# The first projection tile computed in two halves of 256 tokens, with its weights loaded after the first token tile

## The chip, the cores and the metric

The kernel runs on one core of a Trainium2 chip. The metric is the device time of one launch in microseconds (us), median of three runs. A core has TensorE (PE; its weight loads are a row of their own, PEld), VectorE (DVE), ScalarE (ACT), GpSimd (POOL) and SyncE (SP). Each works through its own instructions in order and meets the others only at semaphores. SP here does nothing but issue DMAs.

## The reference

One layer of a decoder trunk on 512 tokens of width 1024. The stretch that the change touches is the very beginning: the norm of x and the first columns of the combined input projection.

```python
def rms_norm(x, g):
    xf = x.astype(jnp.float32)
    y = xf * lax.rsqrt(jnp.mean(xf * xf, axis=-1, keepdims=True) + NORM_EPS)
    return (y * g.astype(jnp.float32)).astype(x.dtype)
...
        h = rms_norm(x, norm_pre_mix[l])
        proj = h @ w_in[l]
        p_rwkv, p_nsa, p_swa, p_gate = _split(proj, (RWKV_COLS, NSA_COLS, SWA_COLS, GATE_COLS))
```

Behind it come three token mixers, an output projection, and a SwiGLU network. All of that is the same before and after.

## The kernel before

**Numbers.** Every dense product is done in three passes. A float32 operand is split into a high part (rounded to the matmul's format) and a low part (the rest): weights WRAW into WHI and WLO, the scaled and transposed x into HHI and HLO. A projection tile is 128 output columns for all 512 tokens: 8 chunks k of the inner dimension, and for each chunk WHI x HHI ("x_high"), WHI x HLO ("x_low") and WLO x HHI ("low"), 24 matmuls in all, which add up in one bank of PSUM. `steps(n)` issues n chunks' worth (3 matmuls each) of the list of tiles, JOBS.

**x.** x arrives as four tiles of 128 tokens (XTOK0[:, t], 512 KB each, semaphore x_in[t]). PE transposes each in 8 blocks of 128x128 (`x_transpose(t, k)`, a product with the identity that lies in CONP). Chunk k of all four token tiles fills bank k of PSUM. The norm's 1/rms is not applied here but to the results, so the products can start on unnormalised x. ACT then writes HHI[k] = high part of (bank k times the gain g_pre_mix), DVE writes HLO[k] = the rest, both 128x512 (ACT L904, DVE L1462), and PE multiplies.

**The gains** come as rows (PRAW) and are turned into columns by two transposes and two DVE copies (L1457, L1458) into PARC. ACT and DVE need them before the first HHI and HLO (semaphore prow_ok).

**Sums of squares** for the norm: x tiles 0 and 2 on ACT (L894), 1 and 3 on DVE (L1452); then a square root, a reciprocal (L1467), four small products (L1469), and one PE product (L2358) that stands in the middle of projection tile 1.

**Order on the queues.** SP issues x tiles 0, 1, 2, then the weights of projection tile 0, then x tile 3, then the weights of tile 1 and small constants. PE transposes tiles 0 to 2 (7 of 8 blocks each), the gains, then 10 transposes of the identity that nobody reads (KEEP_BUSY, they keep the engine working while x tile 3 is on its way), then tile 3, then the eighth block of all four, then the 24 matmuls of tile 0. ACT makes the high part of tile 0's weights (L888), POOL the low part (L773); for tile 1 POOL makes both (POOL_HI, L777). DB[0] and DB[1] (banks 0 and 1) hold the projection tiles in turn, R is the other six banks.

## Time and profile before

| | |
|---|---|
| three runs | 1001.74, 1001.81, 1001.84 us, median 1001.81 |
| profiled execution | 1001.6 us, of it the span between first and last instruction 999.8 us |
| PE busy | 983.0 us (98% of the span) |
| DVE, POOL, ACT busy | 692.9, 452.3, 425.5 us |
| first matmul of projection tile 0 | 14.95 us after the span's start |
| first matmul of projection tile 1 | 20.50 us |

A profile's row names line, engine, operation, output<-inputs and shape. A busy PE says little by itself, since matmuls are pipelined: what counts is when each batch of them starts, and what released it. The change lies in the first 21 us.

### The profile page before, as it was taken

The page shows a single profiled execution, that of the slowest core. Times are in us where ns is not written, and L with a number is a line of the kernel's source. Part 1 is how long each engine was busy: PE and PEld are TensorE (multiplying, and loading weights), DVE is VectorE, ACT ScalarE, POOL GpSimd, SP SyncE. Part 2 cuts the span into 40 slices and gives each one's busy share as a digit, 9 for nine tenths or more (in the row PEclk, how much of TensorE's full clock was granted, in tenths as well). Part 3 has the DMA queues.
Part 4 walks back from the last instruction along what each step waited for, and adds up shares of the span by engine and source line. Part 5 has one row for each costly group of instructions (what it writes and reads, how often), then busy time and mean ns, then how long its engine had stood idle before and what let it go on. Part 6 is the DMA issues. An engine that isn't in the chain of part 4 may idle for free.

```text
span 999.8 us, 19627 instructions
## 1 busy us (share of the span) xinstructions
PE 983.0 (98%) x7920; PEld 799.7 (80%) x7920; DVE 692.9 (69%) x1160; ACT 425.5 (43%) x829; POOL 452.3 (45%) x511
## 2 busy tenths in 40 slices
PE   6999999999999999999999999999999999999997
PEld 5787777777777777777778888888889998888886
DVE  3799796565566956546556882269887865489987
ACT  4134432322314334546555444545444443345563
POOL 3366557254334766656683448446222234510000
PEclk9999999999999999999999999999999999999999
DMA  9345533122223564112113636433322333244452
GB/s 262 89 129 151 122 92 68 24 65 65 67 66 98 157 159 137 49 50 56 52 54 122 193 116 229 131 127 106 106 85 86 112 106 109 86 136 170 157 176 99
DMA packets 149459, 111.48 MB, mean 112 GB/s; under 512 B 21190, under 2 KB 132048, under 8 KB 149369
## 3 DMA queue, kind: packets, MB, share of 16 engines
q1 hardware_dynamic: 145644, 104.16, 35.7%
q10 hardware_dynamic: 3692, 6.07, 2.2%
q8 instruction: 63, 1.03, 0.4%
q14 instruction: 28, 0.22, 0.1%
q0 software_dynamic: 32, 0.00, 0.0%
HBM read 99.70 MB, written 10.52 MB: 110 GB/s over the span
## 4 chain that ended last, share of the span: by engine, by line
PE 86%; DVE 10%; issue 1%; DMA 1%; POOL 1%; ACT 1%; SPq 0%; DVEq 0%; ACTq 0%
PE ps L2318 33%; PE ps L2798 5%; PE ps L2797 5%; PE ps L2802 5%; PE ps L2332 4%; PE ps L2438 3%; PE ps L2683 3%; PE ps L2858 2%; PE ps L2860 2%; PE ps L2859 2%; PE ps L2625 2%; PE ps L2835 2%; PE ps L2832 2%; PE ps L2831 2%; DVE XF L1430 2%
## 5 line engine op out<-in xcount | busy, mean ns | idle before, releaser
L2318 PE MATMUL ps<-HLO,WHI 128*128 128x512 f32 x440 | 178.2, 405 | 0.4 <-issue 0.4
L2318 PE MATMUL ps<-HHI,WHI 128*128 128x512 f32 x440 | 175.5, 399 | 1.0 <-DVE HLO L1462 0.7
L773 POOL TENSOR_TENSOR WLO<-WRAW,WHI 128x1024 fp32r<-128x1024 f32 (+1 forms) x52 | 104.2, 2006 | 106.5 <-ACT WHI L888 106.5
L869 POOL TENSOR_TENSOR WLO<-WRAW,WHI 128x512 fp32r<-128x512 f32 x50 | 72.3, 1453 | 118.8 <-ACT WHI L1230 117.5
L2318 PE MATMUL ps<-HHI,WLO 128*128 128x512 f32 x440 | 118.1, 398 | 0.0
L777 POOL CAST WHI<-WRAW 128x256 fp32r<-128x256 f32 (+1 forms) x133 | 62.7, 472 | 106.5 <-PE ps L2318 106.3
L808 POOL TENSOR_TENSOR WLO<-WRAW,WHI 128x256 fp32r<-128x256 f32 x132 | 105.6, 800 | 10.7
L2318 PEld LDWEIGHTS ps<-HHI,WHI 128*128 128x128 f32 x440 | 82.6, 188 | 23.2 <-issue 4.7
L2318 PEld LDWEIGHTS ps<-HLO,WHI 128*128 128x128 f32 x440 | 82.6, 188 | 22.7 <-issue 5.1
L2318 PEld LDWEIGHTS ps<-HHI,WLO 128*128 128x128 f32 x440 | 80.5, 188 | 18.3 <-issue 1.4
L2798 PE MATMUL ps<-HLO,WHI 128*128 128x512 f32 x200 | 77.9, 389 | 0.0
L2797 PE MATMUL ps<-HHI,WHI 128*128 128x512 f32 x200 | 77.9, 389 | 0.0
L888 ACT ACTIVATE WHI<-WRAW 128x1024 fp32r<-128x1024 f32 (+1 forms) x51 | 43.5, 854 | 71.7 <-PE ps L2318 67.3
L1073 ACT ACTIVATE EB<-EB,STAT 128x257 f32<-128x257 f32 (+5 forms) x96 | 50.4, 526 | 49.5 <-DVE STAT L1809 42.3
L1230 ACT ACTIVATE WHI<-WRAW 128x512 fp32r<-128x512 f32 x69 | 43.0, 629 | 65.7 <-PE ps L2802 42.1
L2802 PE MATMUL ps<-HHI,WLO 128*128 128x512 f32 x200 | 53.5, 389 | 0.0
L837 POOL TENSOR_SCALAR EB<-EB,STAT,GLT 128x128 f32<-128x128 f32 (+3 forms) x64 | 38.6, 615 | 29.2 <-DVE STAT L1825 29.1
L2802 PEld LDWEIGHTS ps<-HHI,WLO 128*128 128x128 f32 x200 | 37.5, 188 | 7.8
L2797 PEld LDWEIGHTS ps<-HHI,WHI 128*128 128x128 f32 x200 | 37.6, 188 | 7.7
L2798 PEld LDWEIGHTS ps<-HLO,WHI 128*128 128x128 f32 x200 | 37.6, 188 | 7.7
L1832 DVE COPY PTB<-ps 128x512 f32<-128x512 f32 (+3 forms) x36 | 20.6, 572 | 32.2 <-PE ps L2332 32.2
L1809 DVE CUSTOM_DVE_ANT_0 EB<-ps,TB 128x128 f32<-128x128 f32 (+3 forms) x64 | 28.2, 488 | 19.2 <-PE ps L2625 16.9
(517 smaller groups left out, 2404.1 us busy)
## 6 DMA issues: line engine op xcount, KB each, us to landing
WRAW<-in_w_in SPq DMA_DIRECT2D x47, 512.0 KB, 4.4
WRAW<-in_w_gate SPq DMA_DIRECT2D x22, 512.0 KB, 3.8
WRAW<-in_w_up SPq DMA_DIRECT2D x22, 512.0 KB, 3.9
WRAW<-in_w_down SPq DMA_DIRECT2D x19, 512.0 KB, 3.4
spilled<-SQ SPq DMA_DIRECT2D x24, 256.0 KB, 2.4
GATES<-spilled SPq DMA_DIRECT2D x6, 768.0 KB, 4.8
WRAW<-in_w_in SPq DMA_DIRECT2D x16, 256.0 KB, 3.7
WRAW<-in_w_branch SPq DMA_DIRECT2D x32, 128.0 KB, 2.9
```

What stands on the lines that cost most here:

```text
L773: return pool.tensor_tensor(lo[:, 0:chunks, :], WRAW[:, n % NRAW, 0:chunks, :], hi[:, 0:chunks, :].bitcast(F32), ALU.subtract)
L777: return pool.tensor_copy(WHI[:, slot_of(n), k0:k1, :], WRAW[:, n % NRAW, k0:k1, :])
L808: lo = pool.tensor_tensor(WLO[:, slot_of(n), k:k + 2, :], WRAW[:, n % NRAW, k:k + 2, :], WHI[:, slot_of(n), k:k + 2, :].bitcast(F32), ALU. ...
L869: pool.tensor_tensor(lo, raw_half(item[1], item[2]), hi.bitcast(F32), ALU.subtract).then_inc(w_lo, 1)
L888: act.activation(split_of(n)[0][:, 0:width_of(n), :], WRAW[:, n % NRAW, 0:width_of(n), :], ACT.Copy).then_inc(w_hi, 1)
L1073: last = act.activation(EB[:, n % 3, g, cols], EB[:, n % 3, g, cols], ACT.Exp, scale=-1.0, bias=st[:, 0, u:u + 1], accum_out=st[:, 1, u:u ...
L1230: act.activation(item_slot(m)[0], raw, ACT.Copy).then_inc(w_hi, 1)
L2318: last = pe.matmul(DB[g % 2][:, :], (wlo if which == "low" else whi)[:, c, :], lo if which == "x_low" else hi, start=a == 0, stop=a == 3 * ...
L2332: return pe.transpose(dst, src, ident[0:n, 0:n])
L2797: pe.matmul(dst, hi[:, kk, :], HHI[:, k, :], start=k == 0, stop=False)
L2798: pe.matmul(dst, hi[:, kk, :], HLO[:, k, :], start=False, stop=False)
L2802: last = pe.matmul(dst, lo[:, kk, :], HHI[:, k, :], start=False, stop=k == 7)
```

## The change

Projection tile 0 is computed in two halves: columns 0 to 255 (tokens of x tiles 0 and 1), then columns 256 to 511 (x tiles 2 and 3).

- `x_chunk(h, k)` places chunk k of half h: two chunks share a bank (k and k+4), half 0 in banks 2 to 5, half 1 in 6, 7, 1, 2. All HHI and HLO operations become 128x256, 16 on each engine where there were 8 of 128x512. ACT's for k of 4 and more wait for DVE's of k-4 (the bank's other chunk).
- SP issues x tile 0, the weights of tile 0, then x tiles 1, 2, 3, then the weights of tile 1.
- POOL makes the high part of tile 0's weights too (POOL_HI = [0, 1]); ACT no longer does.
- DVE's square of x tile 1 stands behind the gain copies, ACT's square of x tile 2 behind all 16 HHI.
- PE: 8 transposes of x tile 0, the gains, 8 of x tile 1, the 10 idle ones, x_high and x_low of chunks 0 to 4 of half 0, 8 transposes of x tile 2, chunks 5 to 7, the 8 low products of half 0, 8 transposes of x tile 3, and the 24 matmuls of half 1 with 256 columns each.

```diff
@@ -139,7 +139,7 @@
 NRAW, NSPL = 4, 2
 
 PIECE0 = NS0 + 5
-POOL_HI = [1]
+POOL_HI = [0, 1]
 KEEP_BUSY = 10
 
 SPILLED = list(range(SW0, GC0))
@@ -497,6 +497,9 @@
     psum = [nc.alloc_psum_tensor(f"ps{n}", [P, T], F32) for n in range(8)]
     DB, R = psum[0:2], psum[2:8]
     DB4 = [DB[0], DB[1], R[0], R[1]]
+
+    def x_chunk(h, k):
+        return psum[((2, 3, 4, 5), (6, 7, 1, 2))[h][k % 4]][:, 256 * (k // 4):256 * (k // 4) + 256]
 
     def head_cols(n, jj, sink=0):
         w = keys_of(n) + sink
@@ -676,10 +679,11 @@
             def x_tile(t):
                 sp.dma_start(XTOK0[:, t, :], x[t * P:(t + 1) * P, :]).then_inc(x_in[t], 16)
 
-            for t in range(3):
-                x_tile(t)
+            x_tile(0)
             for n in range(FF0):
                 if n == 1:
+                    x_tile(1)
+                    x_tile(2)
                     x_tile(3)
                 if n == 2:
                     sp.dma_start(HOT[:, :], hot).then_inc(hot_in, 16)
@@ -896,12 +900,13 @@
 
             x_square(0)
             act.wait_ge(xsq_ok, 1)
+            act.wait_ge(prow_ok, 2)
+            for h in range(2):
+                for k in range(KC):
+                    act.wait_ge(*((xT_done, KC * h + 2 * k + 2) if k < 4 else (xlo_ok, KC * h + k - 3)))
+                    act.activation(HHI[:, k, 256 * h:256 * h + 256], x_chunk(h, k), ACT.Identity,
+                                   scale=par("g_pre_mix", k)).then_inc(xhigh_ok, 1)
             x_square(2)
-            hi_part(0)
-            act.wait_ge(prow_ok, 2)
-            for k in range(KC):
-                act.wait_ge(xT_done, k + 1)
-                act.activation(HHI[:, k, :], psum[k][:, :], ACT.Identity, scale=par("g_pre_mix", k)).then_inc(xhigh_ok, 1)
             act.wait_ge(xsq_ok, 2)
             act.wait_ge(xsum_ok, 2)
             act.activation(XRINV, XSS, ACT.Sqrt, scale=1.0 / D, bias=EPSC[:, 0:1]).then_inc(norm_std, 1)
@@ -1452,15 +1457,17 @@
                 dve.tensor_tensor_reduce(TMP[:, 0:2, :].rearrange("p a t -> p (a t)"), XTOK0[:, t, :], XTOK0[:, t, :],
                                          1.0, 0.0, ALU.mult, ALU.add, XSS[:, t:t + 1]).then_inc(xsum_ok, 1)
 
+            dve.wait_ge(prow_T, 1)
+            dve.tensor_copy(PARC[:, 0:NPAR1], DB[0][:, 0:NPAR1]).then_inc(prow_ok, 1)
+            dve.tensor_copy(PARC[:, NPAR1:NPAR1 + NPAR2], DB[0][:, P:P + NPAR2]).then_inc(prow_ok, 1)
             x_square(1)
-            dve.wait_ge(prow_T, 1)
-            dve.tensor_copy(PARC[:, 0:NPAR1], R[5][:, 0:NPAR1]).then_inc(prow_ok, 1)
-            dve.tensor_copy(PARC[:, NPAR1:NPAR1 + NPAR2], R[5][:, P:P + NPAR2]).then_inc(prow_ok, 1)
             dve.wait_ge(prow_ok, 2)
-            for k in range(KC):
-                dve.wait_ge(xhigh_ok, k + 1)
-                dve.scalar_tensor_tensor(out=HLO[:, k, :], in0=psum[k][:, :], scalar=par("g_pre_mix", k),
-                                         in1=HHI[:, k, :].bitcast(F32), op0=ALU.mult, op1=ALU.subtract).then_inc(xlo_ok, 1)
+            for h in range(2):
+                for k in range(KC):
+                    cols = slice(256 * h, 256 * h + 256)
+                    dve.wait_ge(xhigh_ok, KC * h + k + 1)
+                    dve.scalar_tensor_tensor(out=HLO[:, k, cols], in0=x_chunk(h, k), scalar=par("g_pre_mix", k),
+                                             in1=HHI[:, k, cols].bitcast(F32), op0=ALU.mult, op1=ALU.subtract).then_inc(xlo_ok, 1)
             dve.wait_ge(xsum_ok, 1)
             x_square(3)
             dve.wait_ge(norm_std, 1)
@@ -2279,10 +2286,6 @@
             def products_of(n):
 
                 ks = range(JOBS[n][3])
-                if n == 0:
-                    late = [("low", k - 2) for k in range(2, len(ks) + 2)]
-                    early = [[("x_high", k), ("x_low", k)] for k in ks]
-                    return early[0] + early[1] + sum(([late[k - 2]] + early[k] for k in ks[2:]), []) + late[-2:]
                 return [(part, k) for k in ks for part in ("x_high", "x_low")] + [("low", k) for k in ks]
 
             def steps(count):
@@ -2309,10 +2312,6 @@
                         for a in range(3 * k, 3 * k + 3):
                             which, c = order[a]
                             hi, lo = rhs(n, c)
-                            if n == 0 and which == "x_low":
-                                pe.wait_ge(xlo_ok, c + 1)
-                            if n == 0 and which == "x_high":
-                                pe.wait_ge(*((xhigh_ok, c + 1) if c else (xlo_ok, 1)))
                             if a == first_low:
                                 pe.wait_ge(w_lo, n + 1)
                             last = pe.matmul(DB[g % 2][:, :], (wlo if which == "low" else whi)[:, c, :],
@@ -2334,25 +2333,51 @@
 
             pe.wait_ge(con_in, 16)
             def x_transpose(t, k):
-                return tr(psum[k][:, t * P:(t + 1) * P], XTOK0[:, t, k * P:(k + 1) * P])
-
-            for t in range(3):
-                pe.wait_ge(x_in[t], 16)
-                for k in range(KC - 1):
-                    x_transpose(t, k)
+                at0 = P * (t % 2)
+                return tr(x_chunk(t // 2, k)[:, at0:at0 + P], XTOK0[:, t, k * P:(k + 1) * P])
+
+            def first_high(h, k):
+                cols = slice(256 * h, 256 * h + 256)
+                pe.wait_ge(xhigh_ok, KC * h + k + 1)
+                pe.matmul(DB[0][:, cols], split_of(0)[0][:, k, :], HHI[:, k, cols], start=k == 0, stop=False)
+                pe.wait_ge(xlo_ok, KC * h + k + 1)
+                pe.matmul(DB[0][:, cols], split_of(0)[0][:, k, :], HLO[:, k, cols], start=False, stop=False)
+
+            def first_low(h, k):
+                cols = slice(256 * h, 256 * h + 256)
+                return pe.matmul(DB[0][:, cols], split_of(0)[1][:, k, :], HHI[:, k, cols], start=False, stop=k == KC - 1)
+
+            pe.wait_ge(x_in[0], 16)
+            for k in range(KC):
+                x_transpose(0, k)
             pe.wait_ge(par_in, 32)
-            tr(R[5][:, 0:NPAR1], PRAW[0:NPAR1, 0, :], NPAR1)
-            tr(R[5][:, P:P + NPAR2], PRAW[0:NPAR2, 1, :], NPAR2).then_inc(prow_T, 1)
+            tr(DB[0][:, 0:NPAR1], PRAW[0:NPAR1, 0, :], NPAR1)
+            tr(DB[0][:, P:P + NPAR2], PRAW[0:NPAR2, 1, :], NPAR2).then_inc(prow_T, 1)
+            pe.wait_ge(x_in[1], 16)
+            for k in range(KC):
+                x_transpose(1, k // 2 + 4 * (k % 2)).then_inc(xT_done, 1)
             for n in range(KEEP_BUSY):
-                tr(psum[n % (KC - 1)][:, 3 * P:4 * P], ident)
+                tr(x_chunk(1, n % 3)[:, 0:P], ident)
+            pe.wait_ge(w_hi, 1)
+            pe.wait_ge(prow_ok, 2)
+            for k in range(5):
+                first_high(0, k)
+            pe.wait_ge(x_in[2], 16)
+            for k in range(KC):
+                x_transpose(2, k)
+            for k in range(5, KC):
+                first_high(0, k)
+            pe.wait_ge(w_lo, 1)
+            for k in range(KC):
+                first_low(0, k)
             pe.wait_ge(x_in[3], 16)
-            for k in range(KC - 1):
-                x_transpose(3, k).then_inc(xT_done, 1)
-            pe.wait_ge(prow_ok, 2)
-            for t in range(4):
-                last = x_transpose(t, KC - 1)
-            last.then_inc(xT_done, 1)
-            steps(8)
+            for k in range(KC):
+                x_transpose(3, k // 2 + 4 * (k % 2)).then_inc(xT_done, 1)
+            for k in range(KC):
+                first_high(1, k)
+                last = first_low(1, k)
+            last.then_inc(dense_done, 1)
+            dense["n"] = 1
             steps(4)
             pe.wait_ge(diag_ok, 4)
             pe.matmul(R[4][:, :], ones, SSUM[:, :], start=True, stop=True).then_inc(norm_ss, 1)
```

How the instructions of three queues stand now. SP before, from its first DMA: XTOK are the x tiles, WRAW the raw weights of a projection tile.

```order
L677 DMA XTOK_83<-in_x 128x1024 x3
L711 DMA WRAW<-in_w_in 128x8x128
L677 DMA XTOK_83<-in_x 128x1024
L711 DMA WRAW<-in_w_in 128x8x128
L685 DMA HOT<-in_hot 33x1024
```

SP after, at the same place:

```order
L680 DMA XTOK_83<-in_x 128x1024
L715 DMA WRAW<-in_w_in 128x8x128
L680 DMA XTOK_83<-in_x 128x1024 x3
L715 DMA WRAW<-in_w_in 128x8x128
L689 DMA HOT<-in_hot 33x1024
```

The first weights moved from the fourth place to the second; x tiles 1 and 2 stand one place later, x tile 3 and everything behind it where it was. PE before, from the third x tile to the first matmuls of projection tile 0 (a transpose is a MATMUL with CONP):

```order
L2332 MATMUL ps<-CONP,XTOK_83 128x128 [waits x_in2]
L2332 MATMUL ps<-CONP,XTOK_83 128x128 x6
L2332 MATMUL ps<-CONP,PRAW 128x74 [waits par_in]
L2332 MATMUL ps<-CONP,PRAW 128x64
L2332 MATMUL ps<-CONP 128x128 x10
L2332 MATMUL ps<-CONP,XTOK_83 128x128 [waits x_in3]
L2332 MATMUL ps<-CONP,XTOK_83 128x128 x6
L2332 MATMUL ps<-CONP,XTOK_83 128x128 [waits prow_ok]
L2332 MATMUL ps<-CONP,XTOK_83 128x128 x3
L2318 MATMUL ps<-HHI,WHI 128x512 [waits xlo_ok,w_hi]
L2318 MATMUL ps<-HLO,WHI 128x512 [waits xlo_ok]
```

PE after, from the second x tile to the second half's first matmuls:

```order
L2331 MATMUL ps<-CONP,XTOK_83 128x128 [waits x_in1]
L2331 MATMUL ps<-CONP,XTOK_83 128x128 x7
L2331 MATMUL ps<-CONP 128x128 x10
L2342 MATMUL ps<-HHI,WHI 128x256 [waits xhigh_ok,prow_ok,w_hi]
L2344 MATMUL ps<-HLO,WHI 128x256 [waits xlo_ok]
...
L2331 MATMUL ps<-CONP,XTOK_83 128x128 [waits x_in2]
L2331 MATMUL ps<-CONP,XTOK_83 128x128 x7
...
L2348 MATMUL ps<-HHI,WLO 128x256 [waits w_lo]
L2348 MATMUL ps<-HHI,WLO 128x256 x7
L2331 MATMUL ps<-CONP,XTOK_83 128x128 [waits x_in3]
L2331 MATMUL ps<-CONP,XTOK_83 128x128 x7
L2342 MATMUL ps<-HHI,WHI 128x256 [waits xhigh_ok]
```

Half 0's products stand between the transposes, so the transposes of x tiles 2 and 3 wait their turn behind products. DVE after, its first operations:

```order
L1461 COPY PARC<-ps 128x74 [waits prow_T,con_in]
L1462 COPY PARC<-ps 128x64
L1457 ISA TMP,MISC<-XTOK_83 128x1024 [waits x_in1]
L1457 ISA MISC 128x1
L1469 SCALAR_TENSOR_TENSOR HLO<-ps,PARC,HHI 128x256 [waits xhigh_ok,prow_ok]
L1469 SCALAR_TENSOR_TENSOR HLO<-ps,PARC,HHI 128x256 [waits xhigh_ok] x15
L1457 ISA TMP,MISC<-XTOK_83 128x1024 [waits x_in3,xsum_ok]
```

The square of x tile 1 (the ISA row) now stands behind the copies and directly ahead of 16 HLO operations.

## Rows read from the trace of the kernel before

**Rows 1.** The page: busy time per engine, the clock's slices, the last chain

```profile
PE 983.0 (98%) x7920; PEld 799.7 (80%) x7920; DVE 692.9 (69%) x1160; ACT 425.5 (43%) x829; POOL 452.3 (45%) x511
PEclk9999999999999999999999999999999999999999
PE 86%; DVE 10%; issue 1%; DMA 1%; POOL 1%; ACT 1%; SPq 0%; DVEq 0%; ACTq 0%
```

**Rows 2.** The chain that ended last, 0 to 24 us: start us, us, what

```profile
2.84 9.93 DMA XTOK<-in_x
...
12.82 0.34 PE ps L2332
...
13.25 0.70 ACT HHI L904
...
14.05 0.76 DVE HLO L1462
...
14.95 8.43 PE ps L2318 x36
```

**Rows 3.** Timeline, SP's queue: start us, us the issue took, queue, line, what

```profile
0.74 1.34 SPq L677 DMA_DIRECT2D XTOK<-in_x  x3
2.12 0.68 SPq L711 DMA_DIRECT2D WRAW<-in_w_in  x1
2.84 2.30 SPq L677 DMA_DIRECT2D XTOK<-in_x  x1
```

**Rows 4.** Timeline, PE's weight loads: start, length of the batch, [idle before <-releaser]

```profile
6.14 1.35 PEld L2332 LDWEIGHTS ps<-CONP,XTOK 128*128 128x128 f32 x7 [6.14 <-DMA CONP<-in_con]
7.93 1.34 PEld L2332 LDWEIGHTS ps<-CONP,XTOK 128*128 128x128 f32 x7 [0.43 <-DMA XTOK<-in_x]
9.64 0.75 PEld L2332 LDWEIGHTS ps<-CONP,XTOK 128*128 128x128 f32 x7 [0.37 <-DMA XTOK<-in_x]
10.36 0.40 PEld L2332 LDWEIGHTS ps<-CONP,PRAW 74*128 74x128 f32 x2
10.83 1.07 PEld L2332 LDWEIGHTS ps<-CONP 128*128 128x128 f32 x10
```

**Rows 5.** Timeline, ACT and POOL: weights of tile 0 and 1

```profile
11.47 1.06 ACT L888 ACTIVATE WHI<-WRAW 128x1024 fp32r<-128x1024 f32 x1 [0.63 <-DMA WRAW<-in_w_in]
...
12.61 2.35 POOL L773 TENSOR_TENSOR WLO<-WRAW,WHI 128x1024 fp32r<-128x1024 f32 x1 [10.64 <-ACT WHI L888]
15.15 1.04 POOL L777 CAST WHI<-WRAW 128x1024 fp32r<-128x1024 f32 x1 [0.19 <-DMA WRAW<-in_w_in]
```

**Rows 6.** Timeline, DVE, 8 to 22 us

```profile
8.04 1.22 DVE L1452 CUSTOM_DVE_ANT_0 TMP<-XTOK 128x1024 f32<-128x1024 f32 x1 [7.13 <-DMA XTOK<-in_x]
...
14.05 5.36 DVE L1462 SCALAR_TENSOR_TENSOR HLO<-ps,PARC,HHI 128x512 fp32r<-128x512 f32 x8 [2.74 <-ACT HHI L904]
19.33 1.21 DVE L1452 CUSTOM_DVE_ANT_0 TMP<-XTOK 128x1024 f32<-128x1024 f32 x1
...
21.19 0.87 DVE L1469 TENSOR_SCALAR SSUM<-CONP,MISC 128x128 f32<-128x128 f32 x4
```

**Rows 7.** Timeline, PE: start of projection tile 1, and the norm's product

```profile
20.50 0.39 PE L2318 MATMUL ps<-HHI,WHI 128*128 128x512 f32 x1
...
23.22 1.02 PE L2358 MATMUL ps<-SSUM,CONP 128*128 128x512 f32 x2
```

**Rows 8.** The same operations with 256 columns at the second norm, 650 to 661 us

```profile
650.99 0.28 PE L2762 MATMUL ps<-HLO,XWHI 128*128 128x256 f32 x1
651.11 0.28 PE L2763 MATMUL ps<-HHI,XWLO 128*128 128x256 f32 x1
...
656.51 3.03 ACT L1163 ACTIVATE HHI<-ps,PARC 128x256 fp32r<-128x256 f32 x8 [3.74 <-PE ps L2332]
...
657.39 3.23 DVE L1909 SCALAR_TENSOR_TENSOR HLO<-ps,PARC,HHI 128x256 fp32r<-128x256 f32 x8 [4.01 <-ACT HHI L1163]
```

**Rows 9.** DMA packets of ACT's queue (q10), 9.00 to 9.25 us: packets, MB, share

```profile
q10 hardware_dynamic: 2, 0.00, 0.9%
```

## The prediction

> **What bounds the kernel now.** I read the page first, for who is busy and what the last chain is made of; then that chain over the first 24 us; then the timelines of SP's queue, PE's weight loads, ACT, POOL and DVE over the same stretch; and last the second norm, near 650 us, where the kernel already does with 256 columns what the change now does at the start. PE is busy for 98% of the span and holds 86% of the last chain [rows 1], so from the first projection tile on, the program runs at PE's pace, and whatever moves the first matmul of projection tile 1 moves the end by about as much. That matmul starts at 20.50 [rows 7]; it is the one number of this prediction. Ahead of it the chain is [rows 2]: x tile 3 is in flight until 12.8, PE transposes, ACT makes HHI from 13.25, DVE HLO from 14.05, PE's products run from 14.95 without a gap. So before, the start hangs on the landing of x tile 3, and then 24 matmuls of 512 columns take 20.50 - 14.95 = 5.55 us, of which half could have been done ahead of it. That is what the change goes for. The question is whether anything else has become later.
>
> **Landings.** The change makes the start hang on x tile 1 instead, since half 0 needs tiles 0 and 1. Before, x tiles 0 to 3 are met at about 6.0, 7.9, 9.6 and 12.8 [rows 2, 4], tile 0's weights at 11.47 and tile 1's at 15.15 [rows 5]. SP's order now has the weights second [rows 3]. The queue delivers in its order and each piece has 512 KB, so I give the places their old times: weights about 8.0, x tile 1 about 9.65, x tile 2 about 11.3, x tile 3 and tile 1's weights as before. In small pieces the weights take a little longer than an x tile (9.64 to 11.47 is 1.83 us, 7.93 to 9.64 is 1.71 [rows 4, 5]), so x tile 1 stands at 9.75. Bounds: 9.3 if the lighter start of the queue helps, 10.1 if the weights delay it as much again. The gains come on ACT's queue, whose last packets pass at about 9.2 [rows 9]; PE wants them at 7.8 now (before: 10.36 [rows 4]). They must be there ahead of x tile 1, and are; at worst this costs 0.2 us.
>
> **Weights.** POOL's cast takes 1.04 us and its low part 2.35 [rows 5]: from 8.1 that gives a high part at 9.2 and a low part at 11.6. PE wants them at 11.6 and near 15. Both are covered; the low part has 3 us to spare. The cast of 1.06 us goes from ACT and costs nothing on POOL, which sat idle.
>
> **Half 0.** DVE's square of x tile 1 comes first: 0.1 after landing and 1.25 us with its read-out (8.04 to 9.27 [rows 6]), so DVE is free at 11.1. ACT has HHI of chunk 0 long before, by my count at 10.3 to 10.9. HLO with 256 columns: 8 of them take 3.23 us [rows 8], the last one counted whole (0.48), so the pitch is 0.39. They halve in width but not in time (5.36 us for 8 of 512 columns [rows 6], pitch 0.66): 16 of them cost 6.3 us of DVE where 8 cost 5.4. The fifth, chunk 4, starts at 11.1 + 4 x 0.39 = 12.7, ends 13.15, and PE has its product 0.16 later (14.05 + 0.74 to 14.95 [rows 2], the row's 0.76 rounded): 13.3. Only now come the 8 transposes of x tile 2, 0.107 each when the clock is up (0.75 us for 7 [rows 4]): 14.2. Chunks 5 to 7, six matmuls at 0.12 [rows 8], with the last HLO ready at 14.5: 14.9. Eight low products: 15.85. Then x tile 3 is transposed, though it has lain there since 12.8.
>
> **Half 1.** From the first transpose to ACT is 0.43 us (12.82 to 13.25 [rows 2]); ACT now waits for two, which adds 0.11: 16.4. From ACT's start to DVE's: 0.88 at the second norm, where DVE waits for two ACT operations (pitch 0.37); one less gives 0.51 [rows 8]: 16.9. DVE starts its eighth at 16.9 + 7 x 0.39 = 19.65, ends 20.13; 0.16 to PE, 0.12 each for x_low and low: projection tile 1 starts at 20.55. Before: 20.50. **The sum is +0.05 us.** What half 0 wins is spent on three things: 1.25 us of DVE's square that stands in the way, 0.9 us more of HLO time, and DVE's idle time between its halves (14.3 to 16.9), in which PE, in order, finishes half 0 before it gives ACT anything to do.
>
> **What is late next.** The norm's product wants DVE's four small operations. They end at 22.06 and PE comes for them at 23.2 [rows 6, 7]. DVE leaves HLO at 20.13 instead of 19.41, so they end at about 22.8: 0.4 us of slack is left, no cost. ACT's square of x tile 2 (1.2 us) now runs at 19.3 and is done ahead of DVE's of tile 3 (21.3). POOL's high part of tile 1 waits for a landing that does not move.
>
> **The clock.** This is the open term. The page shows a granted clock of full speed (2.4 GHz) everywhere [rows 1], yet the first and second batch of 7 transposes take 1.35 and 1.34 us and the third 0.75 [rows 4]: PE starts at about half its pace (the 1.2 GHz level) and rises between 9.3 and 9.6, after 14 transposes with one pause of 0.43 us. Now it does 8 transposes, the gains, and then sits from about 8.3 to 9.75, a pause of 1.4 us that was not there. If it rises all the same by then, the sum stands. If it does not, 8 transposes of x tile 1 end at 11.3 instead of 10.6, which DVE doesn't notice, and the ten idle ones end at 13.2 instead of 11.7. PE then has ten matmuls to catch up on, 1.2 us: 14.4 instead of 13.3, and everything behind moves by 1.1 us. Each further us at the slow pace behind 13.2 costs about half a us more. The ten idle transposes are free at full pace and in the way at half pace.
>
> On this the Trainium skill, "TensorE: Matmul & The Clock Gate", Part 4 (PE-mode transpose), has a rule against the change: transposes do not bring the clock up, since they don't count as PE work in the same way. By it PE would stay slow until its first real matmuls. The third batch [rows 4] speaks against it: only transposes had gone before, and it runs at the fast pitch. So I don't build on the rule, but it would make the slow case the longer one.
>
> **Rivals.**
> 1. The clock comes up late (after the idle transposes begin, by about 14): +1.1 us, up to +1.7, so 1002.9 to 1003.6. For it: the new pause right where the clock used to rise. Against: PE has by then worked about as long as before its pause. Chance 0.27.
> 2. It stays slow through half 0's products, and the kernel is slower by more than 2 us. The point is a rise later than about 15.0: 1.1 + (15.0 - 13.2) / 2 = 2.0. Slow until half 0 is done (8 transposes x 0.19, 24 matmuls x 0.24 by doubling [rows 4, 8] from 13.2 make 20.5 instead of 15.85) would be +4.7, 1006.5. Also here: x tile 1 landing beyond 10.5 together with rival 1. Chance 0.12.
> 3. x tile 1 lands early (9.3) and the hand-overs between engines are somewhat shorter than I took them: -0.5 to -1, 1000.9 to 1001.4. Chance 0.10.
> 4. DVE doesn't have to wait between its halves, so that it is bound by itself: 11.1 + 15 x 0.39 + 0.48 = 17.4, plus 0.4: projection tile 1 at 17.8, a gain of 2.7 us, 999.1. PE's order speaks against it: x tile 3's transposes stand behind all of half 0. It would need PE to be far ahead of DVE there, and the row pitches don't give that. Chance 0.06.
>
> **How the numbers follow.** The profiled execution took 1001.6 us, 1.8 of it outside the span of 999.8; the median of three is 1001.81, 0.2 above it. 1001.81 + 0.05, with a term of 0.05 for the gains' wait: 1001.9. That is no change, with 0.45, and its own range is 1001.4 to 1002.4 (x tile 1 at 9.3 or 10.1 is -0.4 or +0.35). For 8 in 10 I take in rival 3 and most of rival 1: 1000.9 to 1003.5. A measurement here can tell about 0.2%, or 2 us, from no change. Faster than 999.8: rival 4, 0.06. Slower than 1003.8: rival 2, 0.12. Within: 0.82.
>
> **What would show it.** Right: x tile 1's transposes start near 9.7; DVE's first HLO near 11.1 and its ninth near 16.9, with an idle gap of over 2 us between eighth and ninth that ends on ACT; x tile 3's transposes start near 15.9 without waiting for a DMA; projection tile 1 near 20.5; the norm's product waits for nothing. The clock: a batch of 8 transposes of x tile 1 in 0.85 us says it is up, 1.5 us says it is not. Wrong: DVE's ninth HLO before 15.5 or after 18.5; a wait of PE for w_lo or w_hi; a wait for the gains that holds up x tile 1; or a shift at 20.5 us that differs from the one at the end by more than 0.5 us, which would mean that the rest of the program does not follow PE's start.

## The result: slower by a quarter of a per cent

| | before | after |
|---|---|---|
| median of 21 runs | 1001.81 us | 1004.56 us |
| lowest to highest | 1001.14 to 1002.97 | 1002.16 to 1006.05 |
| ratio, 95% interval | | 1.0024, 1.0018 to 1.0030 |
| profiled execution, span | 1001.6, 999.8 us | 1006.05, 1004.2 us |

The forecast was 1001.9 with a range of 1000.9 to 1003.5, so the measured time lies outside. It has the size of rival 2 (slower by more than 2 us, 0.12), but not its mechanism, as the clock will show. The profiled execution of after is its slowest of 21; more than half of the loss in its trace is not in every run, as will be seen. The times of after spread over 3.9 us where those of before spread over 1.8, and they gather in two places: ten between 1002.2 and 1004.0, eleven between 1004.6 and 1006.1.

The page of after differs from before's [rows 1] by 24 matmuls and by little else:

```profile
PE 986.5 (98%) x7944; PEld 803.7 (80%) x7944; DVE 696.3 (69%) x1168; ACT 425.7 (42%) x836; POOL 452.6 (45%) x512
```

The timeline has it. First DVE and POOL of after, 8 to 22 us (start us, us, engine, line; in brackets the idle time before and what ended it):

```profile
9.55 3.30 DVE L1457 CUSTOM_DVE_ANT_0 TMP<-XTOK 128x1024 f32<-128x1024 f32 x1
12.78 0.08 DVE L1457 DVE_READ_ACCUMULATOR2_ANT MISC<- 128x1 f32 x1
12.78 3.22 DVE L1469 SCALAR_TENSOR_TENSOR HLO<-ps,PARC,HHI 128x256 fp32r<-128x256 f32 x8
18.68 3.24 DVE L1469 SCALAR_TENSOR_TENSOR HLO<-ps,PARC,HHI 128x256 fp32r<-128x256 f32 x8 [2.68 <-ACT HHI L907]
```

```profile
8.30 1.03 POOL L781 CAST WHI<-WRAW 128x1024 fp32r<-128x1024 f32 x1 [6.33 <-DMA WRAW<-in_w_in]
9.42 2.35 POOL L777 TENSOR_TENSOR WLO<-WRAW,WHI 128x1024 fp32r<-128x1024 f32 x1
```

DVE's square of x tile 1 took 3.30 us where the same operation took 1.22 before [rows 6]. It was issued 0.13 us behind POOL's subtraction, which ran from 9.42 to 11.77, and ended about 1.1 us behind that one's end: it looks as if it had begun only when POOL was done. A later run speaks for that reading: with 9 tiny transposes ahead of x tile 1 (below) the square was issued 0.30 us behind POOL's subtraction instead of 0.13, took 0.17 us less, and ended as long behind POOL's end:

```profile
9.78 3.13 DVE L1457 CUSTOM_DVE_ANT_0 TMP<-XTOK 128x1024 f32<-128x1024 f32 x1
```

```profile
9.48 2.35 POOL L777 TENSOR_TENSOR WLO<-WRAW,WHI 128x1024 fp32r<-128x1024 f32 x1
```

HLO starts at 12.78 instead of the forecast 11.1. Then PE's weight loads of after:

```profile
9.57 1.57 PEld L2331 LDWEIGHTS ps<-CONP,XTOK 128*128 128x128 f32 x8 [0.74 <-DMA XTOK<-in_x]
11.12 2.15 PEld L2331 LDWEIGHTS ps<-CONP 128*128 128x128 f32 x10
13.25 0.34 PEld L2342 LDWEIGHTS ps<-HHI,WHI 128*128 128x128 f32 x1
...
14.54 0.28 PEld L2342 LDWEIGHTS ps<-HHI,WHI 128*128 128x128 f32 x1
14.74 0.19 PEld L2344 LDWEIGHTS ps<-HLO,WHI 128*128 128x128 f32 x1
...
15.11 0.90 PEld L2331 LDWEIGHTS ps<-CONP,XTOK 128*128 128x128 f32 x8
```

Against before's third batch, 7 in 0.75 us [rows 4], these 8 took 1.57 and the idle ten 2.15: PE was at its slow pace (the 1.2 GHz level) until about 14.6, though the page shows the clock as full in every slice. The forecast had one pause of 1.4 us ahead of x tile 1. There are two, of 0.94 us ahead of the gains (7.38 to 8.32) and of 0.74 us ahead of x tile 1 (8.83 to 9.57). There as forecast is DVE's gap between the halves (2.68 us, forecast 2.6). Last, PE of after at the two places that rows 7 show of before:

```profile
22.32 0.40 PE L2317 MATMUL ps<-HHI,WHI 128*128 128x512 f32 x1
...
25.05 1.02 PE L2383 MATMUL ps<-SSUM,CONP 128*128 128x512 f32 x2
```

Projection tile 1 is late by 22.32 - 20.50 = 1.82 us. The span is longer by 4.4. So 2.6 us more arise behind it, and the waits of PE in after (for whom, on whom: us in total, times, longest) between 150 and 320 us say where:

```profile
PE ps L2463 <- issue: 2.3, 5, 0.6
PE ps L2331 <- DVE BK L1656: 0.8, 3, 0.4
```

"issue" is idle time that nothing in the profile ended. Before had two such groups there:

```profile
PE ps L2438 <- issue: 0.7, 2, 0.4
PE ps L2318 <- issue: 0.4, 1, 0.4
```

### The profile page after: what moved, and what is told of

It reads as the page before. It is cut to its first block, busy times and chain, and to the rows that moved or that the text cites. A ratio compares the mean times of both kernels' runs of the same rounds, so it can differ in the third digit from the quotient of the medians.

```text
span 1004.2 us, 19691 instructions
## 1 busy us (share of the span) xinstructions
PE 986.5 (98%) x7944; PEld 803.7 (80%) x7944; DVE 696.3 (69%) x1168; ACT 425.7 (42%) x836; POOL 452.6 (45%) x512
## 4 chain that ended last, share of the span: by engine, by line
PE 86%; DVE 10%; issue 2%; DMA 1%; POOL 1%; ACT 1%; DVEq 0%; SPq 0%; ACTq 0%
PE ps L2317 32%; PE ps L2823 5%; PE ps L2822 5%; PE ps L2827 5%; PE ps L2331 4%; PE ps L2463 3%; PE ps L2708 3%; PE ps L2883 2%; PE ps L2885 2%; PE ps L2884 2%; PE ps L2650 2%; PE ps L2860 2%; PE ps L2857 2%; PE ps L2856 2%; DVE XF L1435 2%
## 5 line engine op out<-in xcount | busy, mean ns | idle before, releaser
L2317 PE MATMUL ps<-HLO,WHI 128*128 128x512 f32 x432 | 175.1, 405 | 0.0
L2317 PE MATMUL ps<-HHI,WHI 128*128 128x512 f32 x432 | 172.3, 399 | 0.3
L2317 PE MATMUL ps<-HHI,WLO 128*128 128x512 f32 x432 | 115.2, 398 | 0.0
L2823 PE MATMUL ps<-HLO,WHI 128*128 128x512 f32 x200 | 77.9, 389 | 0.0
L2822 PE MATMUL ps<-HHI,WHI 128*128 128x512 f32 x200 | 77.9, 389 | 0.0
L2827 PE MATMUL ps<-HHI,WLO 128*128 128x512 f32 x200 | 53.5, 389 | 0.0
```

The source lines that it names most:

```text
L2317: last = pe.matmul(DB[g % 2][:, :], (wlo if which == "low" else whi)[:, c, :], lo if which == "x_low" else hi, start=a == 0, stop=a == 3 * ...
L2822: pe.matmul(dst, hi[:, kk, :], HHI[:, k, :], start=k == 0, stop=False)
L2823: pe.matmul(dst, hi[:, kk, :], HLO[:, k, :], start=False, stop=False)
L2827: last = pe.matmul(dst, lo[:, kk, :], HHI[:, k, :], start=False, stop=k == 7)
```

## The experiments

Two questions: what makes projection tile 1 late (A: DVE and POOL shut each other out; B: PE's slow pace), and what makes the second part. Every kernel was timed beside before on the same chip. When the pace rises is read from the lengths of the weight loads.

### After once more

> The changed kernel again, unaltered, for a second trace of it. If the extra 2.6 us that its first trace shows between 170 and 310 us (PE idle with no releaser, 2.3 us in 5 pauses) belong to the change, they are there again; if they are chance, they differ. Both theories expect the first matmul of projection tile 1 at 22.3 us within 0.3 (20.50 before) and DVE's square of x tile 1 at 3.3 us instead of 1.2.

Measured 1004.27 us (8 runs, 1002.66 to 1005.69), ratio 1.0024 (1.0013 to 1.0034); four runs below 1004, four above. In its trace projection tile 1 starts at 22.24, the square takes 3.31 us, and the span is 1003.7. PE's pauses are there again, in nearly the same places (1.5 us of "issue"). The two traces lose the same at the start and part of the rest. But both were taken in runs of the upper group (1006.05 and 1005.49). Before's median and 1.8 us are 1003.6, and 8 of after's first 21 runs lie below 1003.6, the lowest at 1002.16: those runs lose less at the start, or gain behind it, and no trace shows which.

The pace of this second trace rises at 13.3, not at 14.6, and still projection tile 1 is no earlier. Its x_high loads come at a pitch of 0.39 us, DVE's pitch:

```profile
13.84 0.19 PEld L2342 LDWEIGHTS ps<-HHI,WHI 128*128 128x128 f32 x1
14.12 0.19 PEld L2344 LDWEIGHTS ps<-HLO,WHI 128*128 128x128 f32 x1
14.23 0.19 PEld L2342 LDWEIGHTS ps<-HHI,WHI 128*128 128x128 f32 x1
14.52 0.19 PEld L2344 LDWEIGHTS ps<-HLO,WHI 128*128 128x128 f32 x1
```

PE had caught up there and waited for the late HLO, so A alone holds the start at 22.24.

### The two causes of the late start, each alone and both

POOL's low part of tile 0 waits for DVE's square:

```diff
                 pool.wait_ge(w_hi, n + 1)
+                if n == 0:
+                    pool.wait_ge(xsum_ok, 1)
                 lo_part(n, width_of(n)).then_inc(w_lo, 1)
```

> POOL's low part of tile 0's weights waits until DVE has done its square of x tile 1. Theory A (DVE and POOL exclude each other, the square loses 2.1 us to POOL's subtraction): the square takes 1.22 us again, the first HLO starts at 11.0 instead of 12.8. Theory B (slow TensorE clock): PE never waited for HLO in half 0, since its idle transposes end at 13.3 and its first matmuls run at a pitch of 0.215, so projection tile 1 still starts at 22.3 within 0.3 and the total stays. Were A alone the cause, projection tile 1 would start at 20.6 and the total fall by 1.7 us.

Without the idle transposes:

```diff
-KEEP_BUSY = 10
+KEEP_BUSY = 0
```

> The ten idle transposes are left out. Theory B alone (they are in the way at the slow pace): projection tile 1 about 1 us earlier, at 21.2. Theory A: HLO starts at 12.8 all the same, chunk 4 of half 0 can't be done before 14.9 (15.1 now), so projection tile 1 moves by no more than 0.3 us, unless the clock now rises later and makes it worse.

> Both at once: POOL's low part waits for DVE's square, and no idle transposes. If each alone does nothing because the other bounds, the two together take off 1.2 to 1.8 us: HLO from 11.0, projection tile 1 at 20.5 to 21.1. If the clock stays slow until 14.6 or later, the gain is the smaller one or nothing.

| | square of x tile 1 | first HLO | pace rises | projection tile 1 | median | ratio |
|---|---|---|---|---|---|---|
| after | 3.30 | 12.78 | 14.6 | 22.32 | 1004.56 | 1.0024 (1.0018 to 1.0030) |
| POOL waits | 1.23 | 11.03 | 14.0 | 22.08 | 1003.05 | 1.0016 (1.0008 to 1.0025) |
| no idle transposes | 3.31 | 12.86 | about 18.9 | 24.14 | 1005.26 | 1.0032 (1.0020 to 1.0043) |
| both | 1.23 | 10.99 | 12.6 | 20.43 | 1002.56 | 1.0007 (0.9998 to 1.0016) |

DVE with both edits:

```profile
9.58 1.23 DVE L1459 CUSTOM_DVE_ANT_0 TMP<-XTOK 128x1024 f32<-128x1024 f32 x1
...
10.99 3.23 DVE L1471 SCALAR_TENSOR_TENSOR HLO<-ps,PARC,HHI 128x256 fp32r<-128x256 f32 x8 [0.18 <-ACT HHI L909]
16.80 3.23 DVE L1471 SCALAR_TENSOR_TENSOR HLO<-ps,PARC,HHI 128x256 fp32r<-128x256 f32 x8 [2.58 <-ACT HHI L909]
```

The square is 2.1 us shorter as soon as POOL doesn't subtract beside it: A is shown. By itself it moves the start by only 0.24, as B said: PE comes from its idle transposes at 13.3 and catches up at the slow pace until 14.0, so the finished HLO lie waiting for it. The median is 1.2 us below after's on the same chip (1004.27), of which the start explains 0.2; the rest belongs to the second part, and the two intervals overlap. Without the idle ones alone, projection tile 1 came 1.8 us later than in after, where 0.3 at most, or 1.1 earlier, was expected; the case that the pace rises still later was named there, but without a size. PE sits from 11.5 to 13.4, waiting for the late HLO, and its pace stays slow through nearly all of half 0:

```profile
13.39 0.29 PEld L2344 LDWEIGHTS ps<-HLO,WHI 128*128 128x128 f32 x1 [1.86 <-DVE HLO L1469]
...
15.33 1.66 PEld L2331 LDWEIGHTS ps<-CONP,XTOK 128*128 128x128 f32 x8
```

Eight transposes in 1.66 us at 15.3: that is close to the 4.7 us case of rival 2, here at +3.6. Whether the wait kept the pace slow, one trace can't say. With both edits the wait for HLO is gone too, PE works on from 11.15, and the start is 20.43, before's to 0.07 us. That is what my sum gave for a fast clock (20.55); here the clock was slow until 12.6, but the ten idle transposes were not in its way.

### The clock by itself

Idle transposes for PE in the two pauses ahead of x tile 1, on top of POOL's wait:

```diff
+            for n in range(5):
+                tr(x_chunk(1, n % 3)[:, 0:P], ident)
             pe.wait_ge(par_in, 32)
...
+            for n in range(4):
+                tr(x_chunk(1, n % 3)[:, 0:P], ident)
             pe.wait_ge(x_in[1], 16)
```

> The changed kernel with POOL's low part waiting for DVE's square, and with 5 idle transposes ahead of the gains and 4 ahead of x tile 1, in time that PE waits. Against the kernel with POOL's wait alone (projection tile 1 at 22.1) this shows the clock by itself: if PE's pace rises by 9.6 as in before, the eight transposes of x tile 1 take 0.85 us instead of 1.57, and projection tile 1 starts at 20.5 (within 0.3), a gain of 1.5 us and the number that my sum gave. If the clock was not what held it, it stays at 22.1.

```profile
9.27 0.71 PEld L2333 LDWEIGHTS ps<-CONP 128*128 128x128 f32 x4
9.97 1.45 PEld L2333 LDWEIGHTS ps<-CONP,XTOK 128*128 128x128 f32 x8
11.38 1.12 PEld L2333 LDWEIGHTS ps<-CONP 128*128 128x128 f32 x10
12.47 0.19 PEld L2344 LDWEIGHTS ps<-HHI,WHI 128*128 128x128 f32 x1
```

Projection tile 1 at 20.95, against 22.08 with POOL's wait alone: the pace is worth 1.1 us, the size of my rival 1. The pace rose not at 9.6 but near 11.1, and the four idle transposes held x tile 1 up by 0.4, so it is not the 20.5 expected. Median 1002.4, ratio 1.0003 (0.9994 to 1.0012), with one of the 11 runs, at 3057.8 us, left out: with both causes lightened, no loss can be told from before any more.

This shows what a slow pace costs, and not yet that the pauses make it slow. Seven traces of before and of its padded versions (below) have the same work on PE as far as the gains, and in them the pace rose at 9.5, 9.8, 10.5, 10.6, 10.8, 12.1 and 12.5. The third batch of transposes in two traces of one kernel (24 tiny ones, which come later), whose projection tiles 1 start at 20.71 and 21.64:

```profile
9.73 0.83 PEld L2332 LDWEIGHTS ps<-CONP,XTOK 128*128 128x128 f32 x7 [0.48 <-DMA XTOK<-in_x]
```

```profile
9.63 1.35 PEld L2332 LDWEIGHTS ps<-CONP,XTOK 128*128 128x128 f32 x7 [0.24 <-DMA XTOK<-in_x]
```

With the pauses open it rose at 12.6, 13.3, 14.0, 14.6 and 18.9, with tiny transposes in the second pause alone at 15.4, with both filled at 11.1 here and by 10.3 in the first version below, which points at the pauses. But the last version below had none longer than 0.35 us ahead of x tile 1, and there it rose near 14.4. So that the pauses delay the rise is likely, not shown.

### The second part: PE's pauses

The late start alone, in before: 34 idle transposes instead of 10. Projection tile 1 came 2.1 us late (22.64), and the median is 2.0 above before's beside it (1001.90): one to one, though single runs lie higher.

> The kernel before with 34 idle transposes instead of 10: they run to 14.5, so x tile 3 is transposed 1.65 us late and projection tile 1 starts at 22.1, nearly as in after, and PE's program is as long as that of after. If the late start passes to the end one to one, the total is 1003.5 (+1.65); if the program's length or the lateness itself brings the second part of the loss, it is 1004 to 1004.6 as after's.

Padding alone, in before: tiny transposes in the time that PE waits for x tile 3. The same edit with 12, 24 (on two chips) and 33, and one with 9 in after, ahead of x tile 1:

```diff
                 tr(psum[n % (KC - 1)][:, 3 * P:4 * P], ident)
+            for n in range(24):
+                pe.transpose(psum[n % (KC - 1)][0:32, 3 * P:3 * P + 32], ident[0:32, 0:32], ident[0:32, 0:32])
```

> The kernel before with 24 more tiny transposes (32x32) behind its ten idle ones, in time that PE waits for x tile 3 anyway: PE's program is as long as that of after, its times up to projection tile 1 are those of before (20.5, within 0.3). If the second part of the loss comes from the longer program (instructions fetched at other places), the total rises by 0.5 to 1 us; if not, it stays within 0.3 of before.

> The kernel before with 24 tiny transposes in PE's wait for x tile 3, once more. Theory C (where PE's fetched blocks of instructions begin decides about the pauses): again most runs at 1004 to 1005.2 and a few near 1001.5. If the first result was chance or that chip: one cluster near 1002.

> The same with 12: PE's program is 24 instructions longer than before's. The kernel without idle transposes (28 longer) had one tight cluster whose trace lost nothing behind the start. Theory C: one cluster, 1001.5 to 1002.2, as before. If any padding costs: between 1002.5 and 1004.

> The kernel before with 33 tiny transposes in PE's wait for x tile 3: 66 instructions longer than before, where the kernel with 24 was 48 longer and lay at 1004.1 to 1005.2 in 6 of 9 runs. They last about 1.0 us and may hold projection tile 1 up by 0.3 to 0.5 us. Theory C: 1002.1 to 1002.5, no cluster near 1004.5. If any longer program costs the same, it is 1004.5 again.

> The changed kernel with 9 tiny transposes (32x32) while PE waits for x tile 1. PE's program is 18 instructions longer than after's, 66 longer than before's, as in the kernel with POOL's wait and 9 idle transposes, whose ten undisturbed times had no second cluster. Theory C (the second part of the loss hangs on where in PE's program the fetched blocks of instructions begin): projection tile 1 at 22.3 as in after, but the times lie in one cluster near 1003.4 and the half near 1005.2 is gone. Theory D (it comes from the late start): two clusters as in after, median 1004 to 1004.6.

> The kernel before, unaltered, for a second trace of it. In the first traces the part of the time that arises behind projection tile 1 differs by kernel: after +2.6 and +2.2 us, the one with POOL's wait -0.6, without idle transposes +0.2, with both +0.5. If these pauses of PE (idle, released by nothing that the profile shows) come and go by chance, this trace differs from the first one of before by up to 1 us between 170 and 310 us with projection tile 1 at 20.5 in both; if they are fixed by the program, it doesn't.

In the traces I set the start apart from the rest: "rest" is the span less the start of the norm's product (before: 999.8 - 23.22 = 976.6), "pauses" is PE's "issue" idle between 150 and 320 us.

| kernel | PE instructions more than before | projection tile 1 | rest | pauses | median of all runs, runs above 1004 |
|---|---|---|---|---|---|
| before | 0 | 20.50 | 976.6 | 1.1 | 1001.81, 0 of 21 |
| before, second trace | 0 | 20.41 | 976.4 | 0.8 | 1001.34, 0 of 11 |
| before, 12 tiny | 24 | 20.75 | 978.4 | 1.4 | 1003.15, 2 of 11 |
| before, 24 tiny | 48 | 20.71 | 979.2 | 2.0 | 1004.32, 6 of 9 |
| before, 24 tiny, again | 48 | 21.64 | 979.9 | 2.9 | 1003.22, 4 of 11 |
| before, 33 tiny | 66 | 22.11 | 977.8 | 1.6 | 1002.52, 1 of 11 |
| before, 34 idle | 48 | 22.64 | 975.9 | 0.7 | 1003.94, 5 of 12 |
| after | 48 | 22.32 | 979.2 | 2.3 | 1004.56, 11 of 21 |
| after, second trace | 48 | 22.24 | 978.7 | 1.5 | 1004.27, 4 of 8 |
| after, 9 tiny | 66 | 22.82 | 978.2 | 1.9 | 1003.35, 4 of 11 |
| after, POOL waits | 48 | 22.08 | 976.0 | 0.5 | 1003.05, 3 of 11 |
| after, no idle | 28 | 24.14 | 976.7 | 1.0 | 1005.26, 7 of 7 |
| after, both edits | 28 | 20.43 | 977.0 | 1.3 | 1002.56, 0 of 11 |
| after, POOL waits, 9 idle | 66 | 20.95 | 976.7 | 1.3 | 1002.40, 0 of 10 |
| first version below | 66 | 19.16 | 975.6 | 0.5 | 1000.93, 0 of 10 |
| second version below | 60 | 20.80 | 977.2 | 0.7 | 1001.79, 0 of 11 |

The second trace of the padded kernel, 150 to 320 us, is the clearest:

```profile
PE ps L2440 <- issue: 2.9, 5, 0.9
PE ps L2332 <- DVE BK L1649: 0.9, 2, 0.7
```

What follows. The rest is longer where the pauses are longer, by about 1.8 us for one of pause over these 16 traces; every rest above 977.5 goes with pauses of 1.4 or more. Neither trace of before has them long, and its two rests differ by 0.2. The same kernel with nothing but 12 or 24 tiny transposes ahead has them, with its start late by no more than 0.25 us in two of the three traces, and costs 1.0013 (1.0004 to 1.0022) with 12, and 1.0016 (1.0007 to 1.0026) and 1.0013 (1.0003 to 1.0023) with 24: so neither halves nor a late start are needed for them. In the other trace (21.64) and in that with 33 (22.11) the pace rose at 12.1 and 12.5, so part of those runs' loss is a late start all the same. With 33 the ratio is 1.0007 (0.9998 to 1.0016), no clear loss, though the traced run has pauses of 1.6. A late start with 34 idle transposes mostly gives just the start (1002.4 to 1004.1 in nine of twelve runs), but has three runs of 1005.7 to 1007.3.

Theory C said that 24 instructions more cost nothing, 48 do and 66 don't. Its medians for 66 came true (1003.35 and 1002.52), but both traces have long pauses, 24 instructions cost as much as 48, and POOL's wait at 48 seldom has them: as a rule for the time it is not borne out. Theory D, the late start, fails on the padded kernels. What is shown is that a few tiny transposes more near the start of PE's program can bring up to 3 us between 170 and 310 us, in some runs and not in others. 
I took the pauses for waits for instructions to be fetched. No experiment looked at that, but the traces do: they list DMA packets of a kind "instruction", 16 KB each, on queue q8, 26 or 27 of them in this stretch, about one for every 250 of PE's instructions. Here the longest pause of the second padded trace, and the packets of q8 from 175.5 to 176.9 (packets, MB, share):

```profile
177.09 0.30 PE L2440 MATMUL ps<-AM,XX 64*64 64x64 f32 x8
178.26 0.58 PE L2440 MATMUL ps<-AM,XX 64*64 64x64 f32 x24 [0.88 <-issue]
```

```profile
q8 instruction: 1, 0.02, 5.6%
```

That packet was under way from 175.58 to 176.84, and PE went on 1.42 us later. It is so with every pause: the 16 traces have 43 of 0.2 us and more there that nothing in the profile ended, and each ends 1.19 to 1.64 us after an instruction packet is through, where a moment picked at random would do so in 8 of 100 cases. Their places go with the length of PE's program. Counted from projection tile 1, both traces of before have one at 155.6; the traces with 24 or 28 instructions more have theirs at 151 and 156, or at 156 alone; all four with 66 more have none before 236.7, and the first there. With 48 more there are two kinds, four traces with pauses at 151.1 and 155.7 (after and the kernel with 24 tiny, both traced twice) and two (34 idle, and POOL waits) with pauses at 237 and 278.6 alone. So theory C has the places right, as if they were set by where in the program a packet begins, and not the cost. What is not shown is why some of the fetches come late in one run and not in another.

### A version that tries to beat both

POOL's wait, idle and tiny transposes ahead of the gains and x tile 1, 4 idle ones behind it instead of 10, and PE's order changed so that DVE can go from half 0 to half 1 without its gap. Of its edit, the order:

```diff
+            pe.wait_ge(x_in[2], 16)
+            for k in (0, 4, 1, 5, 2, 6):
+                x_transpose(2, k)
             pe.wait_ge(w_hi, 1)
             pe.wait_ge(prow_ok, 2)
-            for k in range(5):
+            for k in range(2):
                 first_high(0, k)
-            pe.wait_ge(x_in[2], 16)
-            for k in range(KC):
+            pe.wait_ge(x_in[3], 16)
+            for k in (0, 4, 1, 5, 2, 6):
+                x_transpose(3, k).then_inc(xT_done, 1)
+            for k in range(2, 5):
+                first_high(0, k)
+            for k in (3, 7):
                 x_transpose(2, k)
+            for k in (3, 7):
+                x_transpose(3, k).then_inc(xT_done, 1)
...
-            pe.wait_ge(x_in[3], 16)
-            for k in range(KC):
-                x_transpose(3, k // 2 + 4 * (k % 2)).then_inc(xT_done, 1)
```

> A version that means to beat both: POOL's low part waits for DVE's square; short idle transposes keep PE busy ahead of the gains and of x tile 1; six of eight transposes of x tile 2 and of x tile 3 go ahead of most of half 0's products, so that DVE can go on from half 0 to half 1 without its gap of 2.6 us; padded to a program 66 instructions longer than before's. DVE alone would be done with HLO at 17.3; PE has 48 matmuls of 256 columns (5.8 us) and 16 transposes (1.7 us) from 11.2 on, so projection tile 1 starts at 18.7 to 19.6 against 20.5 before, and the total is 1000.0 to 1000.9. If the order of PE's work was not what kept DVE idle, the gap stays and it is 1001.9.

```profile
9.80 1.21 DVE L1459 CUSTOM_DVE_ANT_0 TMP<-XTOK 128x1024 f32<-128x1024 f32 x1
...
11.44 6.36 DVE L1471 SCALAR_TENSOR_TENSOR HLO<-ps,PARC,HHI 128x256 fp32r<-128x256 f32 x16 [0.42 <-ACT HHI L909]
```

```profile
19.16 0.40 PE L2319 MATMUL ps<-HHI,WHI 128*128 128x512 f32 x1
```

All 16 HLO in one run of 6.36 us, projection tile 1 at 19.16, 1.34 before before's. Median 1000.93, ratio 0.9993 (0.9983 to 1.0002): ten runs from 999.2 to 1003.4, and one at 1451.5 that is left out. The second try without idle work just ahead of x tile 1:

> As best1, but the idle transposes ahead of x tile 1 are gone (they held its transposes up until 10.3 although it lands at 9.6) and the padding stands ahead of the gains. If PE's pace rises by 10.5 as in best1, projection tile 1 starts at 18.5 (19.16 in best1) and the total is 0.6 us lower, 1000.3. If the pause ahead of x tile 1 lets the clock rise later, the transposes run at 0.19 and it starts at 19.0 to 19.8, no better than best1.

Measured 1001.79, ratio 0.9995 (0.9985 to 1.0004), from 999.0 to 1002.8; in its trace (of a run of 1002.55) tile 1 starts at 20.80, 1.0 us later than the worst that was expected. PE's pace rises only near 14.4, and DVE waits again between its halves (0.86 and 0.32 us):

```profile
9.08 0.50 PEld L2333 LDWEIGHTS ps<-CONP,PRAW 74*128 74x128 f32 x2
9.70 1.57 PEld L2333 LDWEIGHTS ps<-CONP,XTOK 128*128 128x128 f32 x8
...
14.03 0.33 PEld L2346 LDWEIGHTS ps<-HLO,WHI 128*128 128x128 f32 x1
14.30 0.73 PEld L2333 LDWEIGHTS ps<-CONP,XTOK 128*128 128x128 f32 x6
```

Both beat the changed kernel. That they beat before is likely for the first and not shown for either: the order gains 1.3 us at projection tile 1 in one trace, and in the other trace, with its late clock, nothing of that is left.

## Why the prediction was wrong, point by point

- **What bounds the kernel; the landings.** Right. x tile 1 came at 9.57 (forecast 9.75), the weights at 8.30 (8.0), tile 1's at 14.4 (15.15, earlier than I gave), the gains at 8.3. Nothing waited for weights.
- **"Both are covered": POOL's work on tile 0's weights costs nothing.** This step failed. I asked whether the result was there in time, and not what the operation does to DVE beside it. I put it at nothing. It cost the square 2.1 us and with that the first HLO 1.7, and this alone is enough for the 1.7 us at projection tile 1 (22.24 in the trace whose pace had risen by 13.3). The trace of before had the price, in a stretch that the prediction didn't use. Its chain from 46 us (start, us, what), and POOL there:

```profile
46.13 1.02 DVE XF L1430
...
47.18 2.99 DVE XF L1430
...
50.20 1.01 DVE XF L1430
```

```profile
46.60 2.77 POOL L773 TENSOR_TENSOR WLO<-WRAW,WHI 128x1024 fp32r<-128x1024 f32 x1 [3.04 <-ACT WHI L888]
```

  The same DVE operation takes 1.02 us alone and 2.99 when it meets POOL's subtraction; the one that started first went through. The Trainium skill, "SBUF — State Buffer", section "Who interferes with whom", says it outright: VectorE and GpSimd share one pair of ports, as an exclusive lock held for the whole instruction, and a VectorE operation "with two SBUF inputs" contends with a GpSimd operation that reads SBUF. The square reads x twice, and the operation at 47.18 reads NQ and PARC, which both lie in SBUF: both agree with it. HLO reads PSUM and SBUF, and it was not slowed. In before each takes 0.74 us, beside POOL's subtraction and outside of it. With POOL's wait, HLO and the subtraction start together, and both take what they take alone (8 HLO 3.23 in rows 8, the subtraction 2.35 in rows 5):

```profile
11.03 3.23 DVE L1471 SCALAR_TENSOR_TENSOR HLO<-ps,PARC,HHI 128x256 fp32r<-128x256 f32 x8 [0.18 <-ACT HHI L909]
```

```profile
11.00 2.36 POOL L777 TENSOR_TENSOR WLO<-WRAW,WHI 128x1024 fp32r<-128x1024 f32 x1 [1.60 <-DVE MISC L1459]
```

- **Half 0's and half 1's working.** Right in its pitches and hand-overs: 8 HLO in 3.22 to 3.24, DVE's gap 2.58 to 2.68 for 2.6 where HLO set the pace. The 20.43 with both edits, for 20.55, is in part luck: the pace was slow until 12.6 there and the idle transposes were missing, so it is not the case that was summed up. The order of PE was what kept DVE idle, as rival 4's argument had it: with another order the gap is gone.
- **The clock.** This term failed too. The pace rose at 14.6 and 13.3 in the two traces of after, behind the ten idle transposes both times, and a slow pace measures 1.1 us against the filled pauses. I gave it 0.27 and put the fast case, at nothing, into the sum. It should have been the other way, if only because the kernel itself spent ten transposes on keeping PE at work through a pause. Rival 2's rise beyond 15.0 was in neither trace: A and B together gave its size. The rise also varies, from 9.5 to 12.5 in the seven traces that have before's start. In before that does little harm, since PE waits for x tile 3 until 12.8 anyway. The change moved PE's work to where this variation counts.
- **The rule on transposes**. The Trainium skill, "TensorE: Matmul & The Clock Gate", Part 4 (PE-mode transpose), has it that they don't bring the clock up. In after, the pace rose within the first matmuls; but with filled pauses it rose at 11.1 with nothing but transposes before, and so it did in all seven traces with before's start. The row of before that I set against the rule stands.
- **One to one to the end.** Wrong, and I had named it as what would show me wrong. The late start passes on (34 idle transposes in before: +2.1 at the start, +2.0 in the median), but something that no step of mine had comes on top: the rest is longer by 2.6 and 2.1 us in the two traces of after.
- **The sum.** +0.05 forecast; measured +1.8 and +1.7 at projection tile 1, where POOL's term and the clock's were both nothing in the sum. That each alone gives nearly the whole (22.24 by A, 22.08 by B) is a coincidence of sizes, and both must go for the loss to go. That leaves about +0.9 of the median's +2.75 for what lies behind. The pauses there follow instruction packets; why they differ from run to run stays open.

## What to carry to other kernels

When an operation moves to another engine, ask of both engines' neighbours in time, not only whether the result is there soon enough: the two DVE operations with two SBUF inputs that were issued behind POOL's subtraction, XF before and the square after, ended only behind its end and took 2.0 and 2.1 us more, and a trace that has such a pair has the price. A chain that is moved ahead of the point where everybody waits anyway loses the cover that this wait gave, for the clock's slow start as for the rest; count its pace as slow until a row shows the contrary. A kernel whose pace rises at 9.8 in one trace and at 12.1 in the next needs more than one trace before a cause is named. And time differences of a few tenths of a per cent with a change of the instruction count must be checked against padding alone, and the instruction packets in the list of DMAs looked at.

## What was not expected of the hardware

- DVE's 128x1024 square: 1.22 us alone, 3.30 and 3.31 issued 0.13 us behind a POOL subtraction of 2.35 us, 3.13 issued 0.30 behind it.
- PE's slow pace shows in no clock column, only in durations: 8 transposes in 1.57 us or 0.90, weight loads of 0.33 or 0.19, a pitch of 0.215 or 0.12 for 256 columns. When it ends varied by 3 us among seven traces with the same start.
- 24 tiny transposes in free time made a kernel of 1001.8 us slower by 0.16% and 0.13% on two chips, 12 of them by 0.13%, most of it 150 us and more behind them; 33 of them showed no clear loss.
- Each of 43 pauses of PE between 150 and 320 us that nothing in the profile ended stopped 1.19 to 1.64 us after a 16 KB packet of kind "instruction" had passed.
